# A third PSUM bank for the filling of the first attention, and VectorE's filling cleared at the head of each slot

## The reference, cut to what matters

```python
def swa_mixer(h, w_qkv, sinks, w_o):              # 16 heads of 64, 2 key/value heads, blocks of 128 tokens
    q, k, v = split(h @ w_qkv)
    s = einsum('bnqkgd,bnskd->bnkgqs', q, [k_prev, k]) * HD ** -0.5     # own block and the one before
    logits = where(mask, s - slope * dist, NEG)
    m = maximum(max(logits), sink)
    p = exp(logits - m)
    probs = p / (sum(p) + exp(sink - m))
    o = einsum('bnkgqs,bnskd->bnqkgd', probs, [v_prev, v])
    return o.reshape(B_, T, SWA_HEADS * HD) @ w_o
h = x + swa_mixer(rms_norm(x), ...)
```

## Time and profile before

| what | us |
|---|---|
| median of 3 runs | 2251.18 (2246.56 to 2251.28) |
| the profiled execution, its own time | 2248.18 |
| its span (first to last instruction) | 2246.4 |
| TensorE busy | 2105.2 (94% of the span) |
| VectorE / ScalarE busy | 1307.7 (58%) / 744.2 (33%) |
| mean granted TensorE clock | 0.97 of full speed |

### The profile page before, as it was taken

How to read it: one execution, slowest core, us unless ns; L and a number is a source line. 1 busy time by engine, 2 the same in 40 slices (tenths; PEclk the granted TensorE clock), 3 DMA queues, 4 the chain that set the end, 5 groups by cost and what they waited for, 6 DMA issues and landing times. The chain is left out here.

```text
span 2246.4 us, 26135 instructions
## 1 busy us (share of the span) xinstructions
PE 2105.2 (94%) x10360; PEld 1724.1 (77%) x10360; DVE 1307.7 (58%) x2211; ACT 744.2 (33%) x1387; POOL 193.2 (9%) x170
## 2 busy tenths in 40 slices
PE   5999788999999999999889999789998999999896
PEld 4777667888888888888678888577876778888785
DVE  6277665762562472464578888775354436666634
ACT  4165443421220221222441212362133235444422
POOL 2022220100000000000020000000011002222201
PEclk9999999999999999999989999899999999999998
DMA  3102001231231231231301221115121111011212
GB/s 138 47 25 89 19 20 48 104 112 47 103 104 47 103 111 49 99 108 47 115 28 42 63 93 56 33 57 202 38 98 60 63 61 36 24 36 38 99 48 84
DMA packets 42873, 156.95 MB, mean 70 GB/s; under 512 B 4352, under 2 KB 9088, under 8 KB 41472
## 3 DMA queue, kind: packets, MB, share of 16 engines
q1 hardware_dynamic: 40304, 146.49, 19.5%
q10 hardware_dynamic: 2448, 8.79, 1.0%
HBM read 135.34 MB, written 19.92 MB: 69 GB/s over the span
## 5 line engine op out<-in xcount | busy, mean ns | idle before, releaser
L173 PE MATMUL banks<-u2H,wH 128*128 128x512 f32 x736 | 299.0, 406 | 15.2 <-DVE u2L L367 4.8
L174 PE MATMUL banks<-u2L,wH 128*128 128x512 f32 x736 | 290.9, 395 | 0.0
L175 PE MATMUL banks<-u2H,wL 128*128 128x512 f32 x736 | 290.4, 395 | 0.0
L173 PE MATMUL banks<-aH,wH 128*128 128x512 f32 x640 | 254.4, 397 | 23.7 <-DVE hm L1006 22.2
L175 PE MATMUL banks<-aH,wL 128*128 128x512 f32 x640 | 251.5, 393 | 0.0
L174 PE MATMUL banks<-aL,wH 128*128 128x512 f32 x640 | 251.3, 393 | 0.0
L168 DVE TENSOR_TENSOR wL<-raw,wH 128x1024 fp32r<-128x1024 f32 x153 | 186.6, 1221 | 88.5 <-ACT wH L163 88.5
L163 ACT CAST wH<-raw 128x1024 fp32r<-128x1024 f32 x153 | 159.7, 1045 | 230.7 <-DMA raw<-in_wstream 225.7
L173 PE MATMUL banks<-mH,wH 128*128 128x512 f32 x512 | 200.2, 391 | 0.6 <-DVE mL L369 0.6
L174 PE MATMUL banks<-mL,wH 128*128 128x512 f32 x512 | 199.9, 390 | 0.0
L175 PE MATMUL banks<-mH,wL 128*128 128x512 f32 x512 | 199.9, 390 | 0.0
(11 more groups left out here) (285 smaller groups left out, 4059.4 us busy)
## 6 DMA issues: line engine op xcount, KB each, us to landing
raw<-in_wstream SPq DMA_DIRECT2D x153, 512.0 KB, 3.5
mod_w<-in_mod_w SPq DMA_DIRECT2D x48, 512.0 KB, 5.4
x_scratch<-h SPq DMA_DIRECT2D x2, 4096.0 KB, 11.8
gt<-gates_scratch SPq DMA_DIRECT2D x8, 640.0 KB, 4.6
h<-in_x SPq DMA_DIRECT2D x4, 1024.0 KB, 10.7
hm<-in_x SPq DMA_DIRECT2D x1, 4096.0 KB, 13.5
h<-x_scratch SPq DMA_DIRECT2D x1, 4096.0 KB, 12.4
xo<-x_scratch SPq DMA_DIRECT2D x1, 4096.0 KB, 12.4
```

The lines of the kernel that those rows point to most:

```text
L173: first = pe.matmul(out, aH, bH, start=start, stop=False)
L174: pe.matmul(out, aH, bL, start=False, stop=False)
L175: return first, pe.matmul(out, aL, bH, start=False, stop=stop)
```

## The change

For "swa" alone, the filling rotates over three banks (5, 6, 7) instead of two; to make room, scores get two banks (0, 1), transposes 2 and 3, the output 4, the values' transposes 2 and 3. Waits follow: a filling tile waits for the drain of the third before it. The pace is a little different: the q tiles take 15 slots instead of 14 (2.13 pieces a slot instead of 2.29), and from slot 20 on there are 2 pieces in each slot instead of 2.25. `heads_act` and `heads_dve` read `fill_bank` in the same way. For both attentions, VectorE now also clears its filling at the head of slot i (i > 0) up to the pieces that TensorE had by the end of slot i - 1.

```diff
-                            q_ready=None, factor=lambda st: 1.0):
-            S_RING, T_RING, T_BANK, O_BANK, V_BANKS = 3, 2, 3, 5, (3, 4, 5)
+                            q_ready=None, factor=lambda st: 1.0, rings=(3, 3, 5, (3, 4, 5))):
+            T_RING = 2
+            S_RING, T_BANK, O_BANK, V_BANKS = rings
...
                     for i, slot in enumerate(plan):
                         done = finished(i)
+                        if i:
+                            fill.upto(plan[i - 1].fill)
                         if slot.sums:
                             denominators(slot.k - 1)
...
+        FILL_BANKS = 3
+        def fill_bank(j):
+            return bank(5 + j % FILL_BANKS)
...
-                        if k == 0 and c:
-                            pe.wait_ge(qkv_drained, 4 + 12 + 2 * (c - 1) + ti + 1)
+                        if k == 0 and 2 * c + ti >= FILL_BANKS:
+                            pe.wait_ge(qkv_drained, 4 + 12 + 2 * c + ti - FILL_BANKS + 1)
-                        f, m = mm3(pe, bank(6 + ti), wH[:, u % R, w], wL[:, u % R, w], uH[:, k, TN * ti:TN * ti + TN],
+                        f, m = mm3(pe, fill_bank(2 * c + ti), wH[:, u % R, w], wL[:, u % R, w], uH[:, k, TN * ti:TN * ti + TN],
...
-            pe.sem_inc(wo_drained, 2)
+            pe.sem_inc(wo_drained, FILL_BANKS)
-                        if j < 2:
-                            pe.wait_ge(qkv_drained, 4 + 12 + 6 + j + 1)
+                        if j < FILL_BANKS:
+                            pe.wait_ge(qkv_drained, 4 + 12 + 8 + j - FILL_BANKS + 1)
                         pe.wait_ge(wo_drained, j + 1)
-                    g, m = mm3(pe, bank(6 + j % 2), wH[:, u % R, w], wL[:, u % R, w], aH[:, a, TN * ti:TN * ti + TN],
+                    g, m = mm3(pe, fill_bank(8 + j), wH[:, u % R, w], wL[:, u % R, w], aH[:, a, TN * ti:TN * ti + TN],
...
         def pace1(i):
-            if i < 14:
-                return Q_PIECES * (i + 1) // 14
+            if i < 15:
+                return Q_PIECES * (i + 1) // 15
             if i < 21:
-                return Q_PIECES + 8 * (i - 13) // 7
-            return min(Q_PIECES + 40, Q_PIECES + 8 + (i - 20) * 9 // 4)
+                return Q_PIECES + 8 * (i - 14) // 6
+            return min(Q_PIECES + 40, Q_PIECES + 8 + (i - 20) * 2)
...
-                        factor=lambda st: CG_FACTOR if st[1] else 1.0)
+                        factor=lambda st: CG_FACTOR if st[1] else 1.0, rings=(2, 2, 4, (2, 3)))
```

More of the change, by code:

```diff
@@ L977, in heads_act @@
                     act.wait_ge(qkv_done, 12 + 2 * c + ti + 1)
-                    act.activation(aH[:, 4 + c, TN * ti:TN * ti + TN], bank(6 + ti), ACT.Copy, scale=CG_FACTOR).then_inc(qkv_hi, 1)
+                    act.activation(aH[:, 4 + c, TN * ti:TN * ti + TN], fill_bank(2 * c + ti), ACT.Copy, scale=CG_FACTOR).then_inc(qkv_hi, 1)
                     if ti == 0:
@@ L985, in heads_act @@
                 if v >= 4:
-                    act.wait_ge(wo_drained, 2 + j + 1)
+                    act.wait_ge(wo_drained, FILL_BANKS + j + 1)
                     wo_squares.act(act, j - 16, j % 2, hm[:, 2 * (v % 4) + f, TN * ti:TN * ti + TN], TN)
@@ L994, in heads_dve @@
                     dst = slice(TN * ti, TN * ti + TN)
-                    dve.scalar_tensor_tensor(aL[:, 4 + c, dst], bank(6 + ti), CG_FACTOR, aH[:, 4 + c, dst].bitcast(F32),
+                    dve.scalar_tensor_tensor(aL[:, 4 + c, dst], fill_bank(2 * c + ti), CG_FACTOR, aH[:, 4 + c, dst].bitcast(F32),
                                              ALU.mult, ALU.subtract).then_inc(qkv_drained, 1)
@@ L1005, in heads_dve @@
                 dst = hm[:, 2 * (v % 4) + f, TN * ti:TN * ti + TN]
-                dve.tensor_tensor(dst, bank(6 + j % 2), dst, ALU.add).then_inc(wo_drained, 1)
+                dve.tensor_tensor(dst, fill_bank(8 + j), dst, ALU.add).then_inc(wo_drained, 1)
                 if j == last_tile(v):
```

## The result

| | before | changed |
|---|---|---|
| median of the runs compared, us | 2248.87 (2244.04 to 2251.28, 4 runs) | 2273.99 (2272.89 to 2279.61, 4 runs) |
| ratio, with its 95% interval | | 1.0127 (1.0108 to 1.0146) |
| span of the profiled execution | 2246.4 | 2271.1 |
| TensorE busy | 2105.2 | 2112.2 |

The account below looks back on a forecast made before the run. TensorE, busy 94% of the span, was taken to bound the kernel. Head against third bank 9 (45.2 against 36), clock 13.5, second attention 6.3 and 1.6 sum to 30.4 on 2248.2: 2278 us, range 2258 to 2297.

Parts of the forecast that it names:

- The third bank gives 36: First attention: TensorE's bank waits with restarts (25.2), slow clock (4.1) and low-part waits (6.9) go, 36 us in all.
- The head adds 45.2: First attention: VectorE's early drains and weight splits wait for ScalarE's later copies, so TensorE loses 45.2 us.
- the clock 13.5: First attention: slow matmuls behind nine stalls of 3 to 7 us, 1.5 each, 13.5 us, bounds 0 and 22.
- The 0.7 more in slot 4: First attention, slot 4: scores wait for late logits the same way as in slot 3, 0.7 us lost.
- the short ones: First attention: four short losses, at slots 17, 18, 22 and the last output, 2.0 us together.
- VectorE's new waits some 25 us: First attention: VectorE's new waits on ScalarE at q drains and weight splits (lines 995, 168), some 25 us in all.
- Second attention 6.3 and 1.6: Slot 26: channel 1's last product, moved to the head, waits for the Silu: 6.3 us lost, plus 1.6 slow stretch.
- Two score banks cost nothing, save in slots 3 and 4: First attention: banks taken from the scores cost nothing while VectorE is in time; it decides only in slots 3 and 4.
- Rotation pays, the head is harmless: Rival: early drains wait only for finished things; 29.3 us off, 2219, or 2242 with half of the 45 paid; chance 0.12.
- Both effects, no clock loss: Rival: the stalls come as laid out but the clock holds, 9 + 6.3 = 15 us lost, 2264; chance 0.18.
- The serial form: Rival: ScalarE also waits for VectorE's head, five q slots run in series, some 3 us more each, 2297; chance 0.08.

Follow-up runs that it names:

- the early drain alone: Kernel before plus only VectorE's clearing at the head of the slot, with two filling banks and the old pace: 2275.47 us, ratio 1.0118.
- ScalarE early: The whole change, with ScalarE also clearing its filling at the head of its slot: 2213.39 us, ratio 0.9856 of the kernel before.
- Third bank alone: The whole change without VectorE's clearing at the head (three filling banks, two score banks, new pace): 2208.27 us, ratio 0.9834 of the kernel before.
- the third bank at the old pace: Three filling banks and two score banks, old pace, no clearing at the head: 2214.11 us, ratio 0.9855 of the kernel before.
- only the w drains early: The whole change, but VectorE clears at the head only w-tile drains, nothing in the second attention: 2214.31 us, ratio 0.9862 of the kernel before.
- both engines early with two banks: Kernel before (two filling banks, three score banks, old pace) plus clearing at the head on VectorE and ScalarE: 2216.06 us, ratio 0.9859.
- the one with the drain from slot 16: The whole change, but in the first attention VectorE clears at the head only from slot 16 on: 2252.52 us, ratio 1.0029 of the kernel before.
- the one with the late weight split: The whole change, but VectorE's weight split comes one piece later than the w tile's drain: 2252.61 us, ratio 1.0029 of the kernel before.

## Why the prediction was right

It said 2278 (2258 to 2297) and slower; measured were 2273.99. Its mechanism is shown: the early drain alone gives the changed kernel's waits and time, and taking away only what it waits for (ScalarE early) gives back 60 us. By its steps:

- **The third bank gives 36.** Third bank alone: the stage is 35.2 shorter (287.3 to 252.1), the whole 38.7 by the medians. Inside it the split was off, and 3.1 of it is luck. Idle falls by 24.1 and busy by 11.1. The forecast's waits and restarts were 25.2 and 6.9, 32 in all; what stayed is 4.5 us of short waits (3.5 for the low parts, 1.0 for the logits). With 0.25 for a restart, about 0.16 of which shows as busy, the 12 fewer waits explain 2 of the 11; the rest, 9, is the clock, where I had 4.1. I had counted the two stretches of the earlier trace rows. The trace of before has two more, 12 matmuls from 106.81 and 8 from 258.83 at 0.43 apart. The later one stands behind a wait for a bank (1.87 us), and with the third bank alone it is gone. The earlier one has nothing to do with banks. It lies in the first 8 us of the stage, ahead of every wait for a bank, behind a wait of 3.3 us that all the kernels have there. Those 8 us (columns as above) before, with the third bank alone, and with the third bank at the old pace:

```profile
103.80:111.80 8.00, 8.00 (x30) 6.14 (x30) 1.17 (x8) 0.00 (x0) 0.00 (x0) 0.59 0.21 68
104.00:112.00 8.00, 8.00 (x52) 6.30 (x53) 2.68 (x18) 0.00 (x0) 0.00 (x0) 1.00 0.21 68
102.70:110.70 8.00, 8.00 (x29) 6.07 (x30) 1.17 (x8) 0.00 (x0) 0.00 (x0) 0.57 0.22 68
```

  The same matmuls take some 3.1 us longer at the lower clock. Three traces have 1.00 there (third bank alone, only the w drains early, both engines early with two banks), the other nine 0.57 to 0.59, the changed kernel among them. Without this the bank gives some 32 of the 36, about what it gives by the medians at the old pace (32.9).
- **The head adds 45.2, and the clock 13.5.** From the third bank alone to the changed kernel the stage grows by 56.0 (252.1 to 308.1) where 58.7 were forecast. That these are so close is in part luck: it is 33.8 idle and 22.2 busy. The stalls by the trace, in the order of the prediction's list: 3.02 (3.15), 4.20 (5.7), 3.23 (3.7), 3.24 (3.5), 6.43 (6.9), three of 4.92 or 4.93 (5.4 each), 2.92 (3.3). About 0.2 is to be added to each for the restart, and then all but slot 4 are right to 0.3.

  In slot 4 the chain from neg_max (127.51) to `weigh` is 9.8 us (10.1), but the scores began 0.8 behind neg_max and not 0.1 ahead of it: TensorE itself came late, at the lower clock behind the stall of slot 3.

  The sum of the stalls was some 10 too large: 33.8 idle and about 1.4 of restarts that show as busy, for 45.2. The 0.7 more in slot 4 didn't come, the short ones are 0.8 and not 2.0, and 4.5 us of short waits are there with the third bank alone too.

  The clock term was too small: of the 22.2, 3.1 stand at the stage's start as above and 1.4 are restarts, so that some 17 to 18 are slow matmuls behind the nine stalls, about 1.9 for each and not 1.5.

  Against before, where the stretch at the start cancels, the forecast's terms are 13.3 for waits and restarts (45.2 - (36 - 4.1)) and 9.4 for the clock (13.5 - 4.1); the stage has 9.7 more idle and 11.1 more busy. Each is off by 2 to 4 us, in opposite directions, and the sum by 1.9 (20.8 for 22.7).
- **VectorE's new waits some 25 us.** 46.6. The mis-sized count is of no consequence for the sum, since TensorE's stalls were laid out from the chains; VectorE's waits begin in the idle time that it had before its logits (57.5 us between 100 and 400 before, 40.0 after). TensorE's waits for the low parts were put at about 40: 35.6.
- **Second attention 6.3 and 1.6.** 8.4 in the stage, 10.0 by the run that leaves its early drain out. The one wait (6.11) and the one stall (5.91) are where they were put.
- **Two score banks cost nothing, save in slots 3 and 4.** 0.9996 alone. In slot 3 the scores do wait, 3.02 us for the late logits, but with the early drain only; with the third bank alone two such waits are 0.5 each.
- **Not in the forecast:** the middle of the program is 3.5 shorter. Without that, 24.7 would be 28.2 against 30.4. The change doesn't touch the middle, so this too is luck.

A slow stretch can be read off matmul by matmul. Behind the stall of 6.43 us in slot 15 of the changed kernel:

```profile
220.86 0.80 PE L173 MATMUL banks<-pT1H,vz1H 128*128 128x512 f32 x1 [6.43 <-DVE pT1L L785]
221.46 0.63 PE L174 MATMUL banks<-pT1L,vz1H 128*128 128x512 f32 x1
221.88 0.63 PE L175 MATMUL banks<-pT1H,vz1L 128*128 128x512 f32 x1
229.86 0.39 PE L174 MATMUL banks<-aL,wH 128*128 128x512 f32 x1
230.09 0.39 PE L175 MATMUL banks<-aH,wL 128*128 128x512 f32 x1
```

They start 0.42 apart at first (the 1.2 GHz level) and 0.23 apart from 229.86 on (2.4 GHz).

**The rivals.** *Rotation pays, the head is harmless* had the first half right: third bank alone is 2208, 11 us below its 2219. The head is harmless only if ScalarE moves too (2213). The rule of the Trainium skill that the prediction weighed ("Perfetto Trace Analysis", Optimization Strategy and Matmuls: an even gap points to too little PSUM, and rotating banks lets evacuation and the next group overlap) holds here for the bank, 22.2 us of waits gone (the gap was less even than the prediction says: one of the 12 waits was 0.5 us, the others 1.0 to 3.8). The runs add that an earlier evacuation removes the same gap with the banks as they were. *Both effects, no clock loss* fell by the 0.91. *The serial form* fell as to its price: ScalarE does wait longer for VectorE's neg_max (35.7 us in 10 waits up to 345 us, 14.1 in 11 before), but the stalls of the q slots are no longer than laid out.

**The best version** is the third bank alone, at 0.9834 of before. None of the combinations with early drains that were run was faster.

## What to carry to other kernels

"Finished" has to be asked for every party of a drain, not for the engine that filled the bank: the copy on ScalarE and the reload by DMA were late here, by up to 7 us, while TensorE was long done. An instruction moved to the head of an in-order list takes its waits with it, and all that stood before it pays; price each by what releases it, and move both engines' halves together or neither. A further buffer and an earlier drain are two cures for one gap: try the one that adds no wait first, and don't add up their gains.

## What was not expected of the hardware

From the MLP on, the changed kernel, the one with the drain from slot 16 and the one with the late weight split have the same instructions. The page's windows for that part:

```profile
410.90:2271.10 1860.20, 1774.34 (x8644) 1464.21 (x8644) 1068.39 (x1588) 572.67 (x938) 122.57 (x89) 0.97 0.22 73
387.70:2252.40 1864.70, 1779.83 (x8644) 1468.83 (x8644) 1067.91 (x1588) 572.40 (x938) 122.41 (x89) 0.97 0.22 73
382.40:2250.00 1867.60, 1780.80 (x8644) 1470.11 (x8644) 1069.21 (x1588) 572.60 (x938) 122.39 (x89) 0.97 0.21 72
```

7.4 us lie between them, and 6.5 of these are in TensorE's busy time alone. So which stretches run at the lower clock moves even where nothing was edited, and the first 8 us of the first attention's stage, at 1.00 in three traces and 0.57 to 0.59 in nine behind the same wait, are a second case. What decides it was not tried, and stays open. An edit's price of less than some 7 us is then not to be read from the total, but from its own stage, and there from the matmuls behind the waits that the edit made or removed.
